# Attention with unsplit fp32 probabilities as the stationary operand and 64 columns of v as the moving one

## The reference, cut to what matters

```
s  = einsum('bqhd,bkhd->bhqk', q_i, k) * scale      # per block of 128 queries
pr = softmax(mask_or_bias(s), axis=-1)
o  = einsum('bhqk,bkhd->bqhd', pr, v)
mixed = (o * silu(g)) @ w_out
h = h + mixed
h = h + (p[i] @ pe_w[i]) * sigmoid(rms_norm(h) @ pe_gate_w[i])
```

## Time and profile before

| what | us |
|---|---|
| median of 3 runs (1991.23 to 2003.29) | 1998.39 |
| the profiled execution | 1996.7 |
| its span in the profile | 1994.9 |
| PE busy | 1783.1 (89%) |
| DVE busy | 955.8 (48%) |
| ACT busy | 827.3 (41%) |
| mean granted TensorE clock | 0.956 |

### The profile page before, as it was taken

How to read it: one execution, slowest core, us unless ns; L and a number is a source line. 1 busy time by engine, 2 the same in 40 slices (tenths; PEclk the granted TensorE clock), 3 DMA queues, 4 the chain that set the end, 5 groups by cost and what they waited for, 6 DMA issues and landing times. The chain is left out here.

```text
span 1994.9 us, 31875 instructions
## 1 busy us (share of the span) xinstructions
PE 1783.1 (89%) x12720; PEld 1637.5 (82%) x12720; DVE 955.8 (48%) x1797; ACT 827.3 (41%) x1702; POOL 98.3 (5%) x55
## 2 busy tenths in 40 slices
PE   5999778988996996999989999999968988869998
PEld 5999767867884775999988999998757777769898
DVE  5454556105774665234345444331057777722631
ACT  4433234215773675123153332312157878711410
POOL 0000000000210111000000000000002112100000
PEclk9999989998996998999999999999989999989999
DMA  5054468416424551510123433453174555251111
GB/s 179 22 197 143 119 160 220 122 56 171 127 75 111 138 129 42 184 54 27 49 106 106 127 123 119 131 138 102 45 178 122 142 138 129 64 180 48 64 64 38
DMA packets 178372, 223.94 MB, mean 112 GB/s; under 512 B 12857, under 2 KB 148297, under 8 KB 178225
## 3 DMA queue, kind: packets, MB, share of 16 engines
q1 hardware_dynamic: 177152, 218.43, 38.1%
q0 software_dynamic: 640, 2.62, 0.4%
q10 hardware_dynamic: 432, 0.85, 0.1%
HBM read 150.34 MB, written 77.29 MB: 114 GB/s over the span
## 5 line engine op out<-in xcount | busy, mean ns | idle before, releaser
L1562 PE MATMUL m_acc<-m_w_hi,g_a_hi 128*128 128x256 f32 (+1 forms) x1280 | 370.6, 290 | 19.0 <-DVE m_w_lo L179 14.6
L1562 PE MATMUL m_acc<-m_w_hi,g_a_lo 128*128 128x256 f32 (+1 forms) x1280 | 365.5, 286 | 0.0
L1562 PE MATMUL m_acc<-m_w_lo,g_a_hi 128*128 128x256 f32 (+1 forms) x1280 | 364.6, 285 | 0.0
L1562 PEld LDWEIGHTS m_acc<-m_w_hi,g_a_hi 128*128 128x128 f32 x1280 | 246.0, 192 | 19.4 <-DVE m_w_lo L179 14.7
L1562 PEld LDWEIGHTS m_acc<-m_w_lo,g_a_hi 128*128 128x128 f32 x1280 | 246.8, 193 | 0.0
L1562 PEld LDWEIGHTS m_acc<-m_w_hi,g_a_lo 128*128 128x128 f32 x1280 | 244.6, 191 | 0.0
L611 PE MATMUL pa_acc<-pa_w_hi,g_a_hi 128*128 128x256 f32 (+2 forms) x512 | 156.4, 305 | 15.9 <-DVE pa_w_lo L179 15.9
L1562 PE MATMUL t_acc<-t_w_hi,g_a_hi 128*128 128x256 f32 x512 | 146.9, 287 | 15.2 <-DVE t_w_lo L179 15.2
L611 PE MATMUL pa_acc<-pa_w_hi,g_a_lo 128*128 128x256 f32 (+2 forms) x512 | 151.8, 297 | 0.0
L611 PE MATMUL pa_acc<-pa_w_lo,g_a_hi 128*128 128x256 f32 (+2 forms) x512 | 151.5, 296 | 0.0
L1562 PE MATMUL t_acc<-t_w_hi,g_a_lo 128*128 128x256 f32 x512 | 145.6, 284 | 0.0
(11 more groups left out here) (284 smaller groups left out, 4136.4 us busy)
## 6 DMA issues: line engine op xcount, KB each, us to landing
m_w_raw<-in_fox_w_in SPq DMA_DIRECT2D x16, 1024.0 KB, 6.0
pa_w_raw<-in_ab_w_in SPq DMA_DIRECT2D x10, 1024.0 KB, 5.6
f_v<-m_pr SPq DMA_DIRECT2D x32, 256.0 KB, 2.8
fox_q<-f_q SPq DMA_DIRECT2D x32, 256.0 KB
fox_k<-f_k SPq DMA_DIRECT2D x32, 256.0 KB
fox_v<-f_v SPq DMA_DIRECT2D x16, 512.0 KB, 3.3
s_mq<-pa_xr SPq DMA_DIRECT2D x32, 192.0 KB, 3.0
s_mk<-pa_xr SPq DMA_DIRECT2D x32, 192.0 KB, 3.1
```

Of the source, the lines that this page charges most:

```text
L1562: last = nc.tensor.matmul(dst, a[:, k, t * P:(t + 1) * P], w[:, k0 + k, 0:n], start=(k == 0 and a is m_hi and w is w_hi), stop=(k == kt - ...
```

## The change

In the attention stages v is stored as plain fp32, 64 columns per head and both heads of a pair together; so are the gates, now with tokens on partitions. The transposed probabilities are copied once, unsplit; the copies of successive slots go to ACT and DVE in turn. `times_v` takes one tile at a time: the stationary operand is the 128x128 block of transposed probabilities, the moving one 64 columns of v, both fp32, and the result has queries on partitions. One DVE instruction (`take`) then multiplies by the inverse sum and by the gate. When four tiles of a pair of heads are done, four transpositions (`turn_o`) bring them back to features on partitions through the same `turn` slots, and ACT and DVE write `a_hi` and `a_lo`. `spread_sums`, `take_far`, `take_o` and all of POOL's work in these stages go. The first head's q and k are loaded in two halves. In the projection stages DVE's subtraction for v goes, and a gate unit is computed like q and k: two parts of 24 matmuls, 256 columns each.

```diff
-            v = sp.sb("v", [P, 2, ST, P], F32R)
-            gate = sp.sb("gate", [P, 2, S])
-            gi = sp.sb("gi", [P, S])
-            o = sp.sb("o", [P, 2, S])
-            far = sp.sb("far", [P, 2, NU, 2, 2 * P])
+            v = sp.sb("v", [P, 2, ST, P])
+            gate = sp.sb("gate", [P, 2, ST, P])
+            o = sp.sb("o", [P, 2, ST, P])
...
-            pt_hi = sp.sb("pt_hi", [P, 2, WIDE // P + chk, 2 * P], F32R)
-            pt_lo = sp.sb("pt_lo", [P, 2, WIDE // P + chk, 2 * P], F32R)
+            pt = sp.sb("pt", [P, 3, WIDE // P, P])
...
+                        if hd == 0:
+                            load_qk(0, slice(0, HALF), in_qk[0])
...
+                            load_v(0)
+                            load_qk(0, slice(HALF, S), in_rest)
+                            load_gate(0)
...
+                    def turn_p(g):
+                        _, s, js = ring[g]
+                        lo = lowest(s % NT)
+                        pe.wait_ge(exped, s + 1)
+                        turn_ready(g)
+                        for m, j in enumerate(js):
+                            last = nc.tensor.transpose(turn[:, g % 2, m, :], prob[:, s % 3, (j - lo) * P:(j - lo + 1) * P],
+                                                       ident[:])
+                        last.then_inc(turned, 1)
+
+                    def turn_o(g):
+                        _, m, half = ring[g]
+                        pe.wait_ge(taken, 2 * NT * m + NT + 4 * half + 4)
+                        turn_ready(g)
+                        for n in range(4):
+                            last = nc.tensor.transpose(turn[:, g % 2, n, :], o[:, m % 2, 4 * half + n, :], ident[:])
+                        last.then_inc(turned, 1)
+
+                    def times_v(s):
...
+                        wait(pe, taken, s - 1)
+                        wait(pe, act_copied, act_upto[s])
+                        wait(pe, dve_copied, dve_upto[s])
+                        for j in range(lo, t + 1):
+                            ins = nc.tensor.matmul(pv[:, s % 2, 0:64], pt[:, s % 3, j - lo, :],
+                                                   v[:, m % 2, j, 64 * b:64 * b + 64], start=(j == lo), stop=(j == t))
+                        ins.then_inc(pv_done, 1)
+
+                    for s in steps:
+                        if s < TILES:
+                            score(s)
+                        for g in turns_at[s]:
...
+                        if 0 <= s - 3 < TILES:
+                            times_v(s - 3)
...
+                        if s >= 3:
+                            act.wait_ge(turned, ring_upto[s - 3])
+                        wait(act, inverted, s - 3)
...
+                    def copy_p(g):
+                        _, s, js = ring[g]
+                        dve.wait_ge(turned, g + 1)
+                        wait(dve, pv_done, s - 2)
+                        at = js[0] - lowest(s % NT)
+                        nc.vector.tensor_copy(pt[:, s % 3, at:at + len(js), :], turn[:, g % 2, 0:len(js), :])\
+                            .then_inc(dve_copied, 1)
...
+                    def take(s):
...
+                        dve.wait_ge(inverted, s + 1)
+                        dve.wait_ge(pv_done, s + 1)
+                        nc.vector.scalar_tensor_tensor(out=o[:, m % 2, t, cols], in0=pv[:, s % 2, 0:64],
+                                                       scalar=inverse[:, s % 4:s % 4 + 1], in1=gate[:, m % 2, t, cols],
+                                                       op0=ALU.mult, op1=ALU.mult).then_inc(taken, 1)
...
+                    for s in steps:
+                        if s < TILES:
+                            row_max(s)
+                        if 0 <= s - 2 < TILES:
+                            invert(s - 2)
+                        for g in turns_at[s]:
+                            if g in dve_of:
+                                copy_p(g)
+                            elif g in o_of:
+                                give(g)
+                        if 0 <= s - 3 < TILES:
+                            take(s - 3)
```

More of the change, by code:

```diff
@@ L348, in acc_free @@
                         if ("e", q) in outs_at:
[L349 to L355, removed]
+                            yield out_made, outs_at["e", q] + 1
             def jobs_of(u):
@@ L644, in unit @@
                                 last = tokens(acc[:, banks[u][i], :], c, n, l_hi[:, 3:5], l_lo[:, 3:5], HALF * i, HALF)
-                        elif kind == "v":
+                        else:
                             last = tokens(dst[:, 0:256], c, n, a_hi, a_lo, 0, 256)
[L647 to L654, removed]
                         last.then_inc(summed, 1)
@@ L715, in evacuate @@
                         kind, c, t = units[u]
-                        if kind == "g":
+                        if kind in ("v", "g"):
                             return
[L718 to L731, removed]
                         e = norm_at[u]
@@ L890, in turned @@
             return [js[n:n + cut] for n in range(0, len(js), cut)]
[L892 to L899, removed]
+        steps = range(TILES + 6)
+        turns_at = {s: [] for s in steps}
+        ring = []
+        act_of, dve_of, o_of = {}, {}, {}
+        act_upto, dve_upto, ring_upto = [], [], []
+        for s in steps:
+            if 0 <= s - 2 < TILES:
+                for js in pieces_of((s - 2) % NT):
+                    turns_at[s].append(len(ring))
+                    if (len(act_of) + len(dve_of)) % 2 == 0:
+                        act_of[len(ring)] = len(act_of)
+                    else:
+                        dve_of[len(ring)] = len(dve_of)
+                    ring.append(("p", s - 2, js))
+                act_upto.append(len(act_of))
+                dve_upto.append(len(dve_of))
+                ring_upto.append(len(ring))
+            done = s - 5
+            if done >= 0 and done // NT % 2 == 1 and done % NT in (3, NT - 1):
+                turns_at[s].append(len(ring))
+                o_of[len(ring)] = len(o_of)
+                ring.append(("o", done // NT // 2, done % NT // 4))
+        o_turned = {ring[g][1:]: g + 1 for g in o_of}
         with ExitStack() as st:
@@ L1071, in exp @@
                         act.wait_ge(maxed, s + 1)
-                        if not chk:
-                            wait(act, pieces_turned, piece(s - 2) if s >= 3 else 0)
-                        src = prob[:, s % 3, 0:n] if chk else scores[:, t % 2, 0:n]
+                        if s >= 3:
+                            act.wait_ge(turned, ring_upto[s - 3])
+                        wait(act, inverted, s - 3)
+                        src = prob[:, s % 3, 0:n] if chk else scores[:, s % 2, 0:n]
                         nc.scalar.activation(prob[:, s % 3, 0:n], src, ACT.Exp, bias=neg_max[:, s % 4:s % 4 + 1],
@@ L1099, in give @@
-                    def give(m):
-                        if m < NPAIR - 1:
-                            act.wait_ge(gated, m + 1)
-                        else:
-                            act.wait_ge(last_gated, 2)
-                        nc.scalar.activation(a_hi[:, first_pair + m, :], o[:, m % 2, :], ACT.Copy).then_inc(out_hi, 1)
-                    for s in range(TILES + 5):
-                        if s >= 6 and s % 2 == 0:
-                            take_far((s - 6) // 2)
-                        if 0 <= s - 2 < TILES:
-                            evacuate(s - 2)
+                                             accum_out=total[:, s % 4:s % 4 + 1]).then_inc(exped, 1)
@@ L1143, in evacuate @@
-                    def evacuate(s):
-                        u = s // 2
-                        for n, js in enumerate(turned(s % NT)):
-                            g = piece(s) + n
-                            dve.wait_ge(pt_hi_done, g + 1)
-                            at = js[0] - lowest(2 * (u % NU))
-                            where = (slice(None), u % 2, slice(at, at + len(js)), slice((s % 2) * P, (s % 2 + 1) * P))
-                            nc.vector.tensor_tensor(pt_lo[where], turn[:, g % 2, 0:len(js), :], pt_hi[where].bitcast(F32),
-                                                    ALU.subtract).then_inc(pt_lo_done, 1)
@@ L1587, in unit @@
                                 return
-                        elif kind == "v":
+                        else:
                             last = tokens(dst[:, 0:table[c][1]], c, n, a_hi, a_lo, 0, KD, table[c][1])
-                        else:
-                            w_hi, w_lo = wt.halves(c)
-                            block, cols = slice(n // 2 * P, (n // 2 + 1) * P), slice(n % 2 * HALF, (n % 2 + 1) * HALF)
-                            for k in range(KD):
-                                for w, a in ((w_hi, a_hi), (w_hi, a_lo), (w_lo, a_hi)):
-                                    last = nc.tensor.matmul(dst, w[:, k, block], a[:, k, cols],
-                                                            start=(k == 0 and w is w_hi and a is a_hi),
```

(1 more changed line is left out.)

316 lines of the change are left out of this document (122 added, 194 removed).

## The result

The changed kernel takes 2111.27 us (median of 4 runs, 2108.32 to 2116.53), the kernel before beside it 1996.47 (1991.23 to 2003.29). The ratio is 1.058, interval 1.0535 to 1.0616: slower, as forecast, but by 115 us instead of 26. The profiled execution spans 2107.9 us, against 1994.9.

What follows compares the result with a forecast made beforehand. PE's stream was taken as the floor, with a PE-ACT-DVE-PE loop on top. Heads +46, ends -15, starts -8, projections +4 and -1 made +26 on 1996.7: 2022 us predicted, 1.2% slower, 8-in-10 range 1915 to 2075.

Steps and rivals of the forecast that it cites:

- x: PE's cost of one fp32 product with v in the attention stages, taken as 0.24 us because two weight loads show.
- B: Rival for the products with v: the load hides, x is 0.12, time 1927 us; chance 0.26.
- C: Rival for the products with v: one kind of load hides, x about 0.18, about 1965 us; chance 0.12.
- D: Rival for the products with v: switching between halves costs too, x 0.30 to 0.36, 2088 to 2154 us; chance 0.10.
- E: Rival for the products with v: x 0.06, DVE would bound fox, whole near 1890 us; chance 0.06.
- the 0.22 that the prediction names as its sign of being wrong: Bound on the product with v: the kernel gets faster, and the forecast is wrong, if x is below 0.22.
- That sum: All stages: heads +46, stage ends -15, starts -8, projections +4 and -1, in all +26 us.
- The loop PE-ACT-DVE-PE: Attention stages: PE waits for slots through ACT and DVE; opening it saves 2.2 us a head in fox, 1.0 mla, 1.4 chk.
- Ends and starts: Attention stages: ends shrink from 15.6 to 10.6 us, -15 in all; half loads start sooner, -2.7 a stage, -8.
- Projections: Projection stages: 32 gate units as 48 narrower matmuls cost +4 us; lighter DVE and smaller stores of v give -1.
- chk +2.4, less 1.4: +1.0, eight heads, +8: Heads of chk: PE's stream grows 2.4 us, 1.4 of idle time goes, +1.0 a head, +8 us.

## Why the prediction was right or wrong

**x, and the loads.** Right in kind: two loads for one fp32 product, and 64 columns hide neither. Rivals B, C, D and E are out. The size was 0.24 for a measured 0.21, which takes 1104 x 0.027 = 30 us off the sum, if 0.213 is taken. It is also below the 0.22 that the prediction names as its sign of being wrong. The Trainium skill's estimate (TensorE: Matmul & The Clock Gate, LDWEIGHTS) of 107 ns for 128 columns agrees with the 106 ns of a record here, and 32, 64 and 128 moving columns all came near it (0.106, 0.106 and 0.104). Its four passes (FP8 and Floating Point Precision, TensorE Precision Notes) don't price such a product: the trace has two records, and by four passes with hidden loads it would have been 0.12. The prediction's own bound, faster from x below 0.22, gives about the -4 that 26 - 30 makes.

**That sum, at full clock, holds, in part by luck.** The version with 128 columns has the same loads and no stage that stays at half clock: -3.4 us by spans, against -4. By stage (heads with x at 0.213, less 5 for the end and 2.7 for the start) it is -6.8 for -6.2 in chk and -3.5 for -4.0 in fox. But mla is +7.8 for +3.7, and the projections are -0.8 for +3, and these two errors cancel. By head: mla 20.1 for 20.9 - 36 x 0.027 = 19.9, fox 18.0 for 19.0 - 1.0 = 18.0, chk 19.1 for 19.8 - 0.8 = 19.0.

**The loop PE-ACT-DVE-PE opened.** PE's waits for the slots of `turn`, 27.0 us in 260 of fox, are nearly gone: 2.7 us are left in the 240 of fox above, and PE is busy 237.3. The largest wait of DVE that is new is the one for the product, off PE's path:

```profile
DVE fox_o L1139 <- PE fox_pv L1037: 36.1, 35, 1.3
```

DVE has 159.6 x 18.0 / 240 = 12.0 us of work a head, for 13.4 forecast: beneath PE, as said.

**Ends and starts.** Of the changed kernel, the end of mla on DVE and the first score of fox:

```profile
615.33 1.23 DVE L1107 TENSOR_REDUCE mla_neg_max<-mla_scores 128x1 f32<-128x1024 f32 x1 [1.22 <-PE mla_scores L994]
...
626.29 0.69 DVE L1121 TENSOR_TENSOR g_a_lo<-mla_turn,g_a_hi 128x512 fp32r<-128x512 f32 x1 [1.38 <-ACT g_a_hi L1077]
```

```profile
1568.38 0.47 PE L994 MATMUL fox_scores<-fox_k,fox_q 128*128 128x128 f32 x1 [10.31 <-DMA fox_kx<-s_cum]
```

The end takes 626.98 - 615.33 = 11.7 us, for 10.6 forecast and 15.6 before. Fox's first score comes 6.0 us after its first load at 1562.35, before it was 10.0: 4.0 gained, of which PE gives up to 1.0 back at tile 4. Forecast were -2.7.

**Projections.** Forecast +3, measured +0.6 for `pa`, -3.0 for `m` and +1.0 for `t`. PE's wait in `m` for DVE's `m_w_lo` went from 14.6 to 10.4 us and one of 4.5 for `m_pr` is gone; I had put the lighter DVE at -1.

**The step that failed** is "chk +2.4, less 1.4: +1.0, eight heads, +8". It counted PE's time by durations at full clock and took for granted that the clock stays where it was. The stage ran at 0.50 throughout: 33.7 us a head instead of the 19.1 that it takes with 128 columns and full clock. 14.6 x 7 is 102 us in seven of the eight heads, of the 103.7; the first head is at half clock in the kernel before too. Outside chk the stages sum to +9.3 for +25.7 forecast. The smaller x takes 864 x 0.027 = 23 off that, to +2.4; what is above it is mla, +11.8 for +3.7. Half of those 8 us are the late rise of its clock, since the version with 128 columns, where it rose as early in the stage as before, has +7.8; the other half isn't explained. The forecast of slower came true by luck: without the clock in chk there is no difference. None of the rivals named the clock. The earlier trace rows had the hint, 0.93 in chk against 1.00 in mla and fox. Part of it is the start of the stage, which ran at 0.50 until about 651 us. The rest is three short falls, at about 685, 723 and 760 us, from each of which the clock came back by itself within some 4 us. The first of them in the trace of before, and the stretch after it:

```profile
684.00:690.00 6.00, 5.32 (x31) 4.84 (x30) 2.82 (x10) 3.31 (x9) 0.00 (x0) 0.72 1.00 213
690.00:722.00 32.00, 30.40 (x196) 23.96 (x194) 21.93 (x62) 23.21 (x58) 7.12 (x3) 1.00 0.43 114
```

**What the runs leave open.** They show two states of one stream of work, what lifted it (v's other 64 columns, 448 further columns a tile, a burst in a full pipeline), and what didn't (a burst ahead of the first tiles, one pass with 64 or 128 columns). At the start of chk every version without a burst ahead of the stage ran at half clock, the one before too; why that one rose by itself in its second head and the changed one did not in eight isn't settled. Nor is what lets the clock fall after a burst ahead of the stage: short tiles and a wait of PE for a load stand close together in the traces above. When a stage rises isn't fixed either: with the same instructions in mla, the clock was at 1.00 from about 475 us on in the changed kernel's trace, and from about 512 on in that of the burst in the third head of chk. That may be what spreads the executions of one kernel; it is seen in these two traces only.

## What to carry to other kernels

An fp32 product with few moving columns costs two loads of its stationary operand: count the loads, and fill them, as the other half of v came free. The clock is a term of the sum: read the granted clock of each stage of before, and give a stage that isn't at 1.00 throughout a rival of its own at half clock. If a stage sits at half clock with TensorE full, try some forty wide matmuls once in the running pipeline, not ahead of it.

## What the runs showed of the hardware that was not expected

A stage of 280 us kept half clock though PE was busy 32.00 of 32.00 us, and the same instructions, lifted once, kept full clock for the remaining 120 us. The Trainium skill (TensorE: Matmul & The Clock Gate, Part 1: The HAM clock gate) has the gate follow how busy the engine has been; taken as the busy time of the records, these rows don't bear it out.

Adding work made kernels faster: 128 for 64 columns in chk took some 100 us off, 48 matmuls in one tile some 90.

At full clock a load of 128 columns and the matmul behind it took 0.104 to 0.106 us for 32, 64 and 128 moving columns alike, at half clock 0.20 for 64.
